# Hybrid decoder trunk with expert retrieval: another order for the first passes' steps, TensorE's weighted rows split in two parts of a turn, and more rows added by VectorE

## The reference

```python
h = rms_norm(x, norm_mix[layer]); z = h @ w_in[layer]          # IN_WIDTH = 2564 columns
# four groups of heads on slices of z: forgetting attention, dilated attention,
# differential attention, and a diagonal state-space mixer (S5)
x = x + concat(fox_o, dil_o, diff_o, s5_o) @ w_out[layer]
x = x + peer(rms_norm(x, norm_ffn[layer]), ...)

def peer(xc):                                                  # 128 tokens at a time
    q = (xc @ wq).reshape(c, 8, 2, 128)                        # 8 heads, two halves
    sc = einsum('thpd,hpkd->thpk', q, keys)                    # 128 keys per half
    top_v, top_i = top_k(sc, 16)                               # "best"
    best_v, best_pos = top_k(all 256 pair sums, 16)            # "pairs"
    ids = expert ids of the 16 best pairs per head             # "ids"
    act = gelu(xc . u_tab[ids]) * softmax(best_v)
    return sum over 8 * 16 experts of act * v_tab[ids]
```

## Time and profile before

| | us |
|---|---|
| median of 3 runs (lowest, highest) | 1573.01 (1569.9, 1574.76) |
| the profiled execution, its own time | 1573.96 |
| its span in the trace | 1572.2 |
| TensorE busy | 1375.0 (87%) |
| VectorE busy | 1155.2 (73%) |
| ScalarE busy | 454.9 (29%) |
| GpSimd busy (issuing gathers) | 605.7 (39%) |
| moved by DMA | 627.87 MB, mean 399 GB/s |

### The profile page before, as it was taken

The page is one execution under the profiler, slowest core; times in us unless marked ns, Lnnn a source line. Parts: engine busy times, 40 slices in busy tenths (PEclk is TensorE's granted clock), DMA queues, the critical chain, the costliest instruction groups (busy, mean ns, idle before and its releaser), DMA issues.

```text
span 1572.2 us, 15089 instructions
## 1 busy us (share of the span) xinstructions
PE 1375.0 (87%) x4622; PEld 747.1 (48%) x4622; DVE 1155.2 (73%) x2745; ACT 454.9 (29%) x1096; POOL 605.7 (39%) x525
## 2 busy tenths in 40 slices
PE   8899999999696997988888699999879787877877
PEld 4668445654473443544365245555437433333333
DVE  6929989787688886874668887886658987665555
ACT  3523244343211233342122134343112222121112
POOL 1003345444243334553434334544443443333332
PEclk9989999999798998998999899999989899899899
DMA  9548999999999999999999999999999999999998
GB/s 355 224 147 343 422 421 421 405 417 421 423 402 422 422 402 405 422 420 422 421 418 419 420 415 417 421 394 383 421 423 421 410 406 421 421 422 420 423 420 341
DMA packets 89820, 627.87 MB, mean 399 GB/s; under 512 B 10081, under 2 KB 11361, under 8 KB 20750
## 3 DMA queue, kind: packets, MB, share of 16 engines
q0 software_dynamic: 74144, 537.97, 83.0%
q1 hardware_dynamic: 15598, 88.95, 14.0%
HBM read 625.82 MB, written 1.06 MB: 399 GB/s over the span
## 4 chain that ended last, share of the span: by engine, by line
PE 45%; DMA 30%; DVE 15%; issue 6%; ACT 3%; POOL 1%; SPq 0%; DVEq 0%; ACTq 0%
DMA ring<-table_uv,ids 29%; PE ps L1765 25%; DVE ring L1360 6%; PE ps L1729 5%; PE ps L1529 3%; PE ps L1480 2%; PE ps L1696 2%; PE ps L1519 1%; ACT diag L868 1%; ACT acts L843 1%; PE ps L1596 1%; POOL ring L1829 1%; PE ps L1781 1%; PE ps L1606 1%; DVE weights L1369 1%
## 5 line engine op out<-in xcount | busy, mean ns | idle before, releaser
L1765 PE MATMUL ps<-ring,diag 128*128 128x512 f32 x1884 | 893.8, 630 | 173.7 <-ACT diag L868 169.9
L1829 POOL DMA_INDIRECT ring<-table_uv,ids x512 | 600.0, 1172 | 931.9 <-PE ps L1765 776.9
L1765 PEld LDWEIGHTS ps<-ring,diag 128*128 128x128 f32 x1884 | 372.0, 202 | 644.8 <-issue 636.1
L1360 DVE CUSTOM_DVE_ANT_0 ring<-ring,h 128x1024 f32<-128x1024 f32 x384 | 456.0, 1223 | 150.9 <-DMA ring<-table_uv,ids 148.0
L843 ACT ACTIVATE acts<-dots,small 128x4 f32<-128x4 f32 x126 | 37.5, 297 | 883.0 <-DVE dots L1360 856.6
L1360 DVE CUSTOM_DVE_ANT_0 ring<-ring,ps 128x1024 f32<-128x1024 f32 x120 | 144.6, 1220 | 98.9 <-DMA ring<-table_uv,ids 98.6
L868 ACT ACTIVATE diag<-cst,weights 128x128 f32<-128x128 f32 x471 | 151.4, 390 | 29.1 <-DVE weights L1369 28.9
L1729 PEld LDWEIGHTS ps<-hT,W 128*128 128x128 f32 x896 | 101.9, 192 | 3.5 <-issue 2.9
L1729 PE MATMUL ps<-hT,W 128*128 128x128 f32 x896 | 103.0, 275 | 0.2 <-ACT hT L710 0.2
L1529 PE MATMUL ps<-W,hT 128*128 128x512 f32 (+2 forms) x160 | 60.1, 529 | 1.3 <-DVE hT L991 1.3
L1696 PE MATMUL ps<-W,hT 128*128 128x512 f32 x128 | 57.3, 593 | 0.8 <-DVE hT L1205 0.8
(11 more groups left out here) (322 smaller groups left out, 1217.4 us busy)
## 6 DMA issues: line engine op xcount, KB each, us to landing
W<-peer_wq SPq DMA_DIRECT2D x9, 2048.0 KB, 13.0
W<-w_out SPq DMA_DIRECT2D x6, 2048.0 KB, 13.2
W<-w_in SPq DMA_DIRECT2D x8, 1282.0 KB, 10.9
ring<-table_uv,ids POOLq DMA_INDIRECT x512, 13.1
W<-w_in SPq DMA_DIRECT2D x8, 898.0 KB, 10.5
W<-peer_wq SPq DMA_DIRECT2D x12, 512.0 KB, 12.9
W<-w_in SPq DMA_DIRECT2D x8, 768.0 KB, 9.4
W<-w_in SPq DMA_DIRECT2D x8, 514.0 KB, 12.1
```

Of the source, the lines that this page charges most:

```text
L1360: v.tensor_tensor_reduce(ring_u[:, r, :], ring_u[:, r, :], tokens, 1.0, 0.0, ALU.mult, ALU.add, dots[:, s:s + 1]).then_inc(dots_done, 1)
L1765: mm = pe.matmul(ps[:, c, :], diag[:, s, :], ring_v[:, r, c * 512:(c + 1) * 512], start=(k == 0), stop=(k == SLOTS - 1), skip_group_check= ...
L1829: gp.indirect_dma_start(ring[:, place(t), :], None, table_uv, bass.IndirectOffsetOnAxis(ap=ids[:, b, k:k + 1], axis=0)).then_inc(pair_in[p ...
```

## The change

There are six parts.

1. `FIRST_PLACES` gives the first eight gathers their places, and `PLACES` with `FRESH` the rest: gathers 8 to 11 now reuse the places of gathers 0 to 3, and the fresh places 0 and 1 (freed by query 2) go to gathers 12 and 13. Before, gathers 8 and 9 took them.
2. Query 1 stands ahead of query 5, and `best 5` behind the rows of turn 0. Query 2 stands behind the rows of turn 0, query 3 behind the rows of turn 1; ScalarE copies their results (`queried`) behind "weigh" of turns 1 and 2.
3. In pass 0 the search steps and the projection for pass 1 move back: `best 1`, `best 2`, `best 3` to turns 1, 2, 4, `pairs 2` to turn 5, `ids 2` to turn 6; `rows 0` and `project 0` to turn 3, `project 1` to `3` to turn 4, `project 4` to `7` with `z` in turn 5.
4. From turn 1 on (turn 2 in pass 0), a turn's steps are cut in two halves, and TensorE does the rows of two slots between them and the other rows behind them.
5. Turns 5, 13, 15 and 16 of passes 0 to 2 also give their fourth row to VectorE, 12 more rows in all.
6. The search steps of pass 3 stand in slightly different turns (`spread`).

The diff, cut to its core:

```diff
-PLACES = (7, 2, 3, 4, 5, 6, 8, 9, 0, 1)
+FIRST_PLACES = (7, 2, 3, 4, 5, 6, 8, 9)
+PLACES = (7, 2, 3, 4, 0, 1, 5, 6, 8, 9)
+FRESH = (4, 5)
-ADD_FIRST, ADD_LAST = 20, 30
+ADDED = (5, 13, 15, 16, *range(20, 31))
...
-             [..., "best 4", "pairs 4", "query 5", "score 5", "ids 4", "best 5", "query 1", "score 1"]]
+             [..., "best 4", "pairs 4", "ids 4", "query 1", "query 5", "score 5", "score 1"]]
...
-    inner = [["best 1"], ["rows 0", "best 2"], ["project 0", "best 3"],
-             ["project 1", "project 2", "project 3", "pairs 1", "ids 1"],
-             ["project 4", "project 5", "pairs 2"],
-             ["row", "project 6", "project 7", "ids 2", "z"]]
+    inner = [[], ["best 1"], ["best 2"], ["rows 0", "project 0", "pairs 1", "ids 1"], ["project 1", "project 2", "project 3", "best 3"],
+             ["row", "project 4", "project 5", "project 6", "project 7", "pairs 2", "z"], ["ids 2"]]
...
+            if n == 0 and i in (1, 2):
+                do([f"queried {i + 1}", f"score {i + 1}"], n)
+            if i == 0 or n == 0 and i == 1:
+                plan.append(("rows of v", n, i))
+            if n == 0 and i < 2:
+                do([f"query {i + 2}"], n)
             if n == 0 and i == 0:
-                do(["pairs 5", "ids 5", "query 2"], n)
+                do(["best 5", "pairs 5", "ids 5"], n)
+            if n == 0 and i == 3:
+                do(mixing[i], n + 1)
+            start = len(plan)
...
+            steps = plan[start:]
+            del plan[start:]
+            cut = (len(steps) + 1) // 2
+            plan.extend(steps[:cut])
+            if i > 1 or n and i:
+                plan.append(("first rows of v", n, i))
+            plan.extend(steps[cut:])
+            if i > 1 or n and i:
+                plan.append(("rest of rows", n, i))
```

60 lines of the change are left out of this document (31 added, 29 removed).

## The result

| | before | changed |
|---|---|---|
| median of the first comparison, us | 1573.01 | 1599.44 (1598.31 to 1611.3, 4 runs) |
| ratio, 95% interval | | 1.0187 [1.015, 1.0225] |
| changed kernel again, with later variants, us | 1572.16 | 1598.25 (5 runs), ratio 1.0169 [1.0149, 1.019] |
| profiled execution, span, us | 1573.96, 1572.2 | 1599.0, 1597.2 |
| TensorE, VectorE busy, us | 1375.0, 1155.2 | 1363.6, 1170.8 |

The change made the kernel 26 us (1.7 to 1.9%) slower; 15 us were forecast. The sign was right, and most steps of the first pass were. The sizes for passes 1 and 2 were too small, and pass 0 came out at its number in part by luck.

What follows compares the result with a forecast made beforehand. The 16 DMA engines were taken to set the time. 1573.96 us plus 12.4 (pass 0), 0 (pass 1) and 2.5 (pass 2) gave 1588.9, so 1588 for the median; its own range 1578 to 1598, 8 in 10 runs 1570 to 1600.

Steps and rivals of the forecast that it cites:

- First gathers: Start of pass 0: earlier gathers and rows of turn 0 fill the 4.0 us of idle DMA at 132 to 152 us.
- The chain up to `z`: Pass 0 up to turn 7: `project 7` ends 10.0 us later, and turn 7's dots start 13.3 us late.
- Added rows and cover, pass 0: Pass 0, turns 7 to 20: added rows make the chain 15.9 us late; less cover, 12.4 us of DMA time are lost.
- near 6: Pass 0, 215 to 345 us: landing near 6 us, with the DMA share clearly below 1, would show the forecast.
- bound without any cover (15.9): Pass 0: the upper bound of the DMA time lost, 15.9 us, if no lead of the transfers hides the chain's delay.
- cover of 3.5 us: Pass 0, 300 to 345 us: landing 3.5 us over its least, taken off the chain's delay of 15.9 us.
- Pass 1 at 0: Pass 1: no net change as transfers are queued, between a gain of 2.3 us and a loss of 3.4 us.
- Pass 2 at 2.5: Pass 2: uncovered waits at turns 1 and 6 lose 2.5 us, bounds 0.5 and 5.7 us.
- the credit set against it: Pass 2: rows given away in turns 13, 15 and 16 (5.2 us) help against the 5.7 us delay.
- The lead lasts: Rival: the chain is not late at `z`, idle times at 132 and 584 us go, 1567 us; chance 0.13.
- cover eats the delay: Rival: the 13.3 us delay is offset by 6.7 us of cover, 4.0 of lead and 2.3 in pass 1; 1573 us, chance 0.13.
- Waits bring the lower clock: Rival: four new waits, each followed by 2.35 us more of rows, add 9.4 us; 1597 us, chance 0.07.

Runs made afterwards that it cites:

- e8: Parts 1, 2 and 6 alone against the kernel before: no cut, no rows added beyond turns 20 to 30, projection in nearly its old turns; 1582.47 us, ratio 1.0047.
- e6: The changed kernel with `ids 2` back ahead of `z` in turn 5 of pass 0; 1593.33 us, ratio 1.0132 to the kernel before.
- e1: The changed kernel without the cut in any pass, the rows of a turn whole behind its steps; 1588.97 us, ratio 1.0098 to the kernel before.
- e9: The changed kernel with the rows of turn 1 whole behind the steps in passes 1 and 2, cut elsewhere; 1599.35 us, ratio 1.0151 to the kernel before.
- e2: The changed kernel with the cut in pass 0 alone, rows whole in passes 1 and 2; 1591.27 us, ratio 1.0121 to the kernel before.
- e12: The kernel before with only the 12 more rows added by VectorE (turns 5, 13, 15, 16 of passes 0 to 2); 1579.31 us, ratio 1.005.
- e14: The changed kernel with 61 idle matmuls ahead of the first rows of 13 turns, to keep TensorE busy; 1598.03 us, ratio 1.0155 to the kernel before.

## Why the prediction was right or wrong

**(1) First gathers.** Right: the share at 132 to 152 us rose to 0.96, and turn 0's rows started at 128.4 us (134 were expected, and 5 us of the difference are the prologue's clock; in e8, whose gathers started as in the kernel before, they stand at 133.97). The gain didn't last: at 60 MB it was 2 to 3 us beyond the early start, and by 90 MB it was gone.

**(2) The chain up to `z`.** Right in its steps for the changed kernel, save one. VectorE of the changed kernel, pass 0 (`z`, then the first dot of turns 6 and 7), to compare with the earlier trace rows:

```profile
214.44 0.75 DVE L1057 TENSOR_SCALAR h<-ps,small 128x512 f32<-128x512 f32 x1 [12.04 <-PE ps L1544]
...
217.03 1.22 DVE L1375 CUSTOM_DVE_ANT_0 ring<-ring,h 128x1024 f32<-128x1024 f32 x1
...
232.28 1.16 DVE L1375 CUSTOM_DVE_ANT_0 ring<-ring,h 128x1024 f32<-128x1024 f32 x1
```

The wait for `z` was 12.04 us (11 forecast). Turn 7's dots at 232.28 are 9.4 us later than before, and 14.5 counted from the earlier start (13.3 forecast). TensorE, to compare with the earlier trace rows:

```profile
144.46 1.16 PE L1764 MATMUL ps<-key_rows,h 128*128 128x128 f32 x8 [1.86 <-ACT h L835]
...
186.15 5.37 PE L1786 MATMUL ps<-ring,diag 128*128 128x512 f32 x8 [2.46 <-ACT diag L883]
...
210.27 6.19 PE L1544 MATMUL ps<-W,hT 128*128 128x512 f32 x16
216.30 1.88 PE L1786 MATMUL ps<-ring,diag 128*128 128x512 f32 x4
...
222.80 9.69 PE L1786 MATMUL ps<-ring,diag 128*128 128x512 f32 x16 [4.40 <-ACT diag L883]
...
312.51 8.80 PE L1786 MATMUL ps<-ring,diag 128*128 128x512 f32 x16 [3.28 <-ACT diag L883]
```

`project 7` ended at 216.4 us, 11.4 late from the start of the gathers (10.0 forecast), and the wait for turn 6's `diag` was 4.40 us (4.8). `score 2` waited 1.86 us (1.9 forecast), the first rows of turn 4 waited 2.46 us (3.1). The step that was left out is the lower clock: those rows then took 5.37 us for 3.60, 1.8 us more, which no term of the sum had. e6 shows the 5.4 us of `ids 2` by themselves. The share of the cut in the 10.0 us, 6.5 by the forecast's terms, was too large: without it (e1) `project 7` is 10.1 us late and not 3.5, as the last chunk of w_in then decides.

**(3) Added rows and cover, pass 0: near the number in part by luck.** The delay was 13.2 us at 160 MB in the one profile and 11.4 in the other, against 12.4. Turn 17's rows, before and in the changed kernel:

```profile
333.05 7.11 PE L1765 MATMUL ps<-ring,diag 128*128 128x512 f32 x16
```
```profile
344.90 10.08 PE L1786 MATMUL ps<-ring,diag 128*128 128x512 f32 x16 [3.60 <-ACT diag L883]
```

They are 11.9 us late, 17.0 from the start of the gathers (15.9 forecast). The landings, to compare with the earlier trace rows (229 to 300 us, 300 to 345 us, all):

```profile
DMA to landing us min/median/max: 5.6/9.2/11.0
...
DMA to landing us min/median/max: 6.2/8.6/12.0
...
DMA to landing us min/median/max: 5.6/12.6/24.9
```

The least is at 5.6 and 6.2 us, about the least of the whole run, so the cover was used up; the medians stayed some 3 us above "near 6". From the start of the gathers pass 0 lost 18.3 us, more than even the forecast's bound without any cover (15.9). So the step that failed in pass 0 is the cover of 3.5 us that was taken off the chain's delay: the runs show none of it. The 12.4 came out only because the gathers started 5 and 7 us earlier in these two profiles, which goes with the prologue's clock. In e9, with the same code in pass 0 and a start only 0.7 us earlier, the delay at 160 MB was 19.9 us.

**(4) Pass 1 at 0: failed.** "Transfers are queued there", and the first rows' wait of 3 us was to be harmless. TensorE of the changed kernel, the first rows of turns 2 and 3:

```profile
554.76 5.37 PE L1786 MATMUL ps<-ring,diag 128*128 128x512 f32 x8 [2.80 <-ACT diag L883]
...
572.00 3.60 PE L1786 MATMUL ps<-ring,diag 128*128 128x512 f32 x8
```

The wait was there (2.80 us), the rows behind it took 1.8 us longer at the lower clock, and neither was harmless. Pass 1 lost 2.8 and 4.7 us in the two profiles, and without a cut in it (e1, e2) it gains 2 to 3 us on the one profile of before, so the cut costs it some 4 to 8. The idle time of the earlier trace rows at 584 to 596 us (2.3 us) came back with the delay at 596 to 612 us, at a share of 0.79 (3.4 us).

**(5) Pass 2 at 2.5: mis-sized.** It lost 7.3 and 6.0 us. The wait was as foreseen; TensorE and ScalarE of the changed kernel, to compare with the earlier trace rows:

```profile
922.80 6.12 PE L1786 MATMUL ps<-ring,diag 128*128 128x512 f32 x8 [6.48 <-ACT diag L883]
...
995.86 8.80 PE L1786 MATMUL ps<-ring,diag 128*128 128x512 f32 x16 [3.11 <-ACT diag L883]
```
```profile
922.26 1.28 ACT L883 ACTIVATE diag<-cst,weights 128x128 f32<-128x128 f32 x4 [0.23 <-DVE weights L1384]
```

6.48 us against 6.3 forecast. What failed is the credit set against it: the 5.2 us of rows given away in turns 13, 15 and 16, which were to help. The added rows help nowhere: in e12 they cost 4.7 us in pass 0, and in pass 2 the kernels with them lost some 2 us more on average than those without. The lower clock behind the wait (6.12 us for 3.60) was not in the sum either. The upper bound of the term, 5.7 us, would have been near the mark.

**Parts.** Built up by the medians: parts 1 and 2 8.7 us, part 3 1.4, part 5 5.8, the cut 10.2; 26.1 in all. The split depends on the order in which they are added: part 5 costs 7.5 us alone and 2.4 last, and parts 1 and 2 alone bring a wait that the changed kernel doesn't have. The forecast had 12.4 of its 14.9 us in pass 0. The two profiles were 25.0 and 22.1 us late. Against the terms they are 0.8 over and 1.0 under in pass 0 (with the early start), 2.8 and 4.7 over in pass 1, 4.8 and 3.5 over in pass 2, and 1.7 and 0.0 over after 550 MB.

**Rivals.** "The lead lasts" and "cover eats the delay" failed at the point named, turn 7's dots. "Waits bring the lower clock" came nearest in its number (1597 us). Its mechanism is seen: the four rows behind the new waits took 1.8 to 2.6 us more each, and in pass 2 that reached turn 6. What share of the 26 us it is stays open, as e14's idle matmuls stand wrong in pass 1. Open as well stays how the cut's cost in turns 1 and 2 to 4 divides; the single profile of each variant and the overlap of the intervals don't settle it to better than 3 us.
